# A two-block sequence model in fp32 precision: the second block's branch gates as seven half-width products per unit, and squares summed before the ones-matmul

## The chip, the cores and the metric

One NeuronCore of a Trainium2 chip runs the whole program as one launch. The metric is the device time of the kernel in microseconds (us), lower is better. TensorE (PE) multiplies, VectorE (DVE) and ScalarE (ACT) do elementwise work, GpSimd (POOL) a little of it, and all weights come over one DMA queue that SyncE (SP) fills in program order.

## The reference, cut to what matters

The model is two blocks of two layers each over 528 (first block) or 512 (second block) tokens, width 1024, all fp32. In a layer of the second block, `h = rmsnorm(x, g)` is projected by `w_in`, and three attention branches give `y_a`, `y_b`, `y_m`. The last 3072 columns of `w_in` are the branch gates:

```python
z = jnp.einsum('bsd,dn->bsn', h, w_in)
dq, dk, dv, dg, lq, lk, lv, lg, mq, mg, mgate = jnp.split(z, splits, axis=-1)
...
gates = jax.nn.sigmoid(mgate).reshape(B, S, N_BRANCH, D_MODEL)
merged = gates[:, :, 0] * y_a + gates[:, :, 1] * y_b + gates[:, :, 2] * y_m
return x + jnp.einsum('bsd,de->bse', merged, w_out)
```

Every RMS norm needs, per token, the sum over 1024 channels of `x*x`.

## The kernel before

**Data.** Activations lie channel by channel: xT, hh and hl are eight tiles of 128 channels by 512 (or 528) tokens. hh is the normed activation rounded to the short matmul format, hl the rest. A weight piece is 128 by 1024 fp32, 512 KB. It is staged by DMA in one of two buffers (st), copied by ACT to a rounded half (ch), and DVE subtracts to give the rest (cl). ch and cl have three buffers each. An fp32 product is three matmuls: ch with hh, ch with hl, cl with hh.

**A unit** is 256 output channels: two pieces, the first with input channels 0 to 511, the second with 512 to 1023. `proj` (L339, engine part L1116) computes 128 output channels by 512 tokens: 8 input tiles x 3 matmuls of 512 columns, so a unit is 48 of them. The gates of one layer are 3 branches x 4 units.

**Order.** `Order` writes one list of steps; every engine walks it in that order and runs its own part of each step, waiting on semaphores. Nothing overtakes on an engine. `weights` (L314) puts the conversion of the next piece: SP issues the DMA of the piece two further on (L2717), ACT waits for the staged piece and for the last matmul that read the buffer three pieces back, DVE waits for ACT. Before a unit starts, both of its pieces are converted; during its first half the next piece is put, and behind the matmuls of its second half the one after.

**The second block's layer** (`block2`, L607): differential attention; then three dilated groups g, each with projections (`lq`, `lk`, `lv`) and at its end four score steps `lS` (L1425, L1860, L2438), in which PE takes two pairs of PSUM banks in turn and DVE reads them; then the joint softmax (`lse0` to `lse2`, `pn`); then memory attention (`fA` scores, `fB` transposes, `fC` values, four times each) between the gates of the branches (`lg`, `mg`); then the stage that the change touches. For c = 0 to 3: gates of branch 0, unit c (`gate`, L735; tanh by ACT, L1939, into one of six TG buffers), two `br` steps with pieces "bd" (24 matmuls each), gates of branch 1 and of branch 2, unit c, and two steps with pieces "bm" (two `br` of 12 matmuls each). `brev` (L2583) multiplies and adds in the merge tile. `o2` is the output projection. At c = 0 the copies `ybs` and `yms` (four each on ACT and on DVE) stand behind the gates of branch 1 and 2.

**Start of the second block's layer.** SP loads three bias tables (`gload`, 448 KB each) behind a barrier; the weight pieces that come later stand behind them in the queue.

**Squares** (`squares`, L353). For the norm sums of the three later norms ACT squares each tile (L1571), and PE multiplies it with a ones matrix in plain fp32 (`sqp`, L1106), eight accumulated steps per norm, one behind each output tile.

```python
def weights(self):
    if self.converted < len(self.plan):
        self.put("w", self.converted)
        self.converted += 1
```

Of the kernel before, what the change touches and what calls it, by code (L numbers as in the profile page):

```python
# [290 lines left out]

class Order:


    def __init__(self):
        self.o, self.plan = [], stream_plan()
        self.taken = self.converted = self.sq = self.g = self.gr = self.tg = self.sw = self.rot = 0
        self.owed = False
# [54 lines left out]
    def squares(self, sid):  # L353
        ns = []

# [251 lines left out]
    def block2(self, l):  # L607
        put, nid = self.put, 2 + l
        put("bar", ("b2", l))
        for h in range(3):  # L610
            put("gload", l, h)
        st = {}
# [32 lines left out]
        for g in range(3):  # L645
# [34 lines left out]
            for i in range(4):  # L680
                put("lS", l, g, i)
        put("bar", ("send", l))
# [16 lines left out]
        put("lse2", l)  # L699
        for g in range(3):  # L700
# [26 lines left out]
        def mg(t):  # L727
# [3 lines left out]
            s = self.nsq()  # L731
            tgs["mg", t] = self.ntg()
            put("mgev", l, t, s, tgs["mg", t])
# [18 lines left out]
        gate(0, 0)  # L752
        put("fB", l, 2)
        gate(0, 1)
# [7 lines left out]
        for c in range(4):  # L762
            if c:
                gate(0, 2 * c)
                gate(0, 2 * c + 1)
            for n in (2 * c, 2 * c + 1):
# [3 lines left out]
                if n == 0:  # L770
                    put("fC", l, 3)
                    for t in range(4):
                        put("ymm", l, t, tgs["mg", t])
            gate(1, 2 * c)
            gate(1, 2 * c + 1)
# [3 lines left out]
            gate(2, 2 * c)  # L779
            gate(2, 2 * c + 1)  # L780
            if c == 0:
                for k in range(4):
                    put("yms", l, k)
            if c == 3:
# [4 lines left out]
            for n in (2 * c, 2 * c + 1):  # L789
# [4 lines left out]
                self.weights()  # L794
        for n in (6, 7):
# [7 lines left out]
        for n in range(8):  # L803
            p = first[n] if n < 2 else self.take(2, l, "out", n)
            put("o2", l, n, p, 6 if n < 2 else 0, 8)
            self.weights()
            put("o2ev", l, n)
# [46 lines left out]
def program(nc, I, out):  # L854
    with ExitStack() as ctx:
# [9 lines left out]
        xT, hh = k8(sb("xT", 8 * L)[:, :]), k8(sb("hh", 8 * L, F32R)[:, :])  # L865
        with nc.sbuf_tensor("hn", [128, 8 * L], F32) as HN:
            pass
        hnf, hl = k8(HN[:, :]), k8(sb("hl", 8 * L, F32R)[:, :])
        ifh, ifl = sb("ifh", 128, F32R), sb("ifl", 128, F32R)
        cst, rot_all = sb("cst", S_W), sb("rot", 2 * L)  # L870
        idb = sb("idb", 128, BF16)
        mskb = sb("mskb", C_W - C_MA, BF16)
# [2125 lines left out]
```

## Time and profile before

| | us |
|---|---|
| median of 3 runs | 3013.37 (3012.73 to 3016.75) |
| the profiled execution | 3014.49 |
| its span in the profile | 3012.7 |
| mean granted TensorE clock | 0.99 |
| PE / DVE / ACT busy | 2913.7 / 1620.4 / 1257.1 |

The span is cut into instructions with start and duration; the number in brackets behind a row is how long the engine had stood idle, and which engine's result ended that. Matmuls overlap one another, so that their durations are longer than their spacing: what one costs is the distance from its start to the next start. The difference of 1.8 us between the execution's own time and its span is launch and end.

### The profile page before, as it was taken

To read this page: it belongs to the slowest core of one execution; us is meant where nothing else is said; L and a number is where in the kernel's file an instruction comes from. 1 tells how busy PE (TensorE), PEld (TensorE's weight loads), DVE (VectorE), ACT (ScalarE), POOL (GpSimd) and SP (SyncE) were. 2 spreads that over 40 slices of the span, in tenths; PEclk is the share of its full clock that TensorE was granted. 3 is DMA by queue.
4 is the path that set the end of the run, shared out by engine and by line. 5 is a ranking of instruction groups with operands and counts; after the bars stand their busy time and mean duration, and the time that the engine had idled before them with its cause. 6 is when DMAs were issued, how large, how long until landed. Compare 5 with 4: busy or idle time off the path is not lost.

```text
span 3012.7 us, 42468 instructions
## 1 busy us (share of the span) xinstructions
PE 2913.7 (97%) x17182; PEld 2492.2 (83%) x17182; DVE 1620.4 (54%) x3205; ACT 1257.1 (42%) x2630; POOL 187.2 (6%) x207
## 2 busy tenths in 40 slices
PE   8899999999999999999999999999999999999998
PEld 7888888988887777898888888887888888888886
DVE  6777545367675454676333654334677433565334
ACT  5455423255553233565334333233566324433222
POOL 2100000020001000100000000000100000000000
PEclk9999999999999999999999999999999999999999
DMA  3111222211113222322232222232322232222222
GB/s 116 52 50 54 101 69 71 85 55 57 52 59 107 69 98 91 109 74 78 84 119 85 76 79 84 91 105 91 115 72 80 79 118 84 80 75 86 97 91 84
DMA packets 99726, 250.07 MB, mean 83 GB/s; under 512 B 8597, under 2 KB 44845, under 8 KB 99274
## 3 DMA queue, kind: packets, MB, share of 16 engines
q1 hardware_dynamic: 99530, 247.35, 25.1%
q8 instruction: 136, 2.23, 0.3%
q14 instruction: 60, 0.49, 0.1%
HBM read 239.60 MB, written 6.50 MB: 82 GB/s over the span
## 4 chain that ended last, share of the span: by engine, by line
PE 82%; DVE 9%; ACT 4%; issue 2%; POOL 1%; DMA 1%; SPq 0%; DVEq 0%; POOLq 0%; ACTq 0%
PE ps L93 79%; PE ps L96 3%; ACT Z L99 2%; DVE Z L102 2%; DVE Z L110 2%; DVE cl L102 1%; ACT ch L99 1%; POOL stat L102 1%; DVE ZR L102 1%; DMA st<-in_stream_dram 1%; DVE Z L106 1%; DVE stat L123 1%; DVE stat L110 1%; DVE Z L120 1%; DVE hn L110 0%
## 5 line engine op out<-in xcount | busy, mean ns | idle before, releaser
L93 PE MATMUL ps<-hl,ch 128*128 128x512 f32 (+1 forms) x2512 | 831.5, 359 | 0.0
L93 PE MATMUL ps<-hh,ch 128*128 128x512 f32 (+1 forms) x2368 | 802.5, 365 | 25.5 <-DVE cl L102 10.7
L102 DVE TENSOR_TENSOR cl<-st,ch 128x1024 fp32r<-128x1024 f32 (+1 forms) x436 | 501.9, 1158 | 594.3 <-ACT ch L99 594.0
L93 PE MATMUL ps<-hh,cl 128*128 128x512 f32 (+1 forms) x2368 | 792.5, 361 | 0.0
L99 ACT ACTIVATE ch<-st 128x1024 fp32r<-128x1024 f32 (+1 forms) x436 | 428.7, 990 | 356.9 <-PE ps L93 323.5
L93 PEld LDWEIGHTS ps<-hh,ch 128*128 128x128 f32 x2368 | 423.0, 190 | 107.6 <-ACT Z L99 15.0
L93 PEld LDWEIGHTS ps<-hl,ch 128*128 128x128 f32 x2512 | 448.7, 190 | 72.6
L93 PEld LDWEIGHTS ps<-hh,cl 128*128 128x128 f32 x2368 | 424.0, 190 | 70.7
L99 ACT ACTIVATE Z<-ps 128x512 f32<-128x512 f32 (+7 forms) x506 | 216.4, 437 | 548.5 <-PE ps L93 442.1
L93 PE MATMUL ps<-ZR,ch 128*128 128x512 f32 (+2 forms) x1680 | 443.1, 353 | 2.0 <-DVE cl L102 1.6
L93 PEld LDWEIGHTS ps<-ZR,ch 128*128 128x128 f32 x1680 | 285.0, 189 | 52.3 <-issue 9.2
L93 PE MATMUL ps<-Z 128*128 128x128 f32 (+8 forms) x1522 | 264.2, 317 | 15.1 <-DVE Z L110 5.0
L93 PEld LDWEIGHTS ps<-Z 128*128 128x128 f32 (+5 forms) x1522 | 201.3, 186 | 68.9 <-issue 37.3
L93 PE MATMUL ps<-ZR,cl 128*128 128x512 f32 (+2 forms) x720 | 234.4, 351 | 0.0
L93 PE MATMUL ps<-ch,hh 128*128 128x256 f32 (+2 forms) x736 | 212.4, 289 | 3.8 <-DVE stat L106 2.0
L93 PE MATMUL ps<-cl,hh 128*128 128x256 f32 (+2 forms) x736 | 208.9, 284 | 0.0
L93 PE MATMUL ps<-ch,hl 128*128 128x256 f32 (+2 forms) x736 | 208.3, 283 | 0.0
L99 ACT ACTIVATE Z<-Z,stat 128x512 f32<-128x512 f32 (+4 forms) x264 | 151.2, 587 | 122.2 <-DVE stat L106 113.1
L93 PE MATMUL ps<-ZR 128*128 128x256 f32 (+4 forms) x1040 | 178.1, 331 | 11.1 <-DVE stat L106 11.1
L96 PE MATMUL ps<-cst,Z 128*128 128x128 f32 (+2 forms) x950 | 147.2, 274 | 8.3 <-DVE Z L102 5.9
L99 ACT ACTIVATE Z<-ps,stat 128x272 f32<-128x272 f32 (+2 forms) x160 | 84.2, 532 | 162.5 <-DVE stat L110 128.8
L93 PEld LDWEIGHTS ps<-ZR 128*128 128x128 f32 (+2 forms) x1040 | 122.7, 189 | 30.9 <-DVE stat L106 12.5
(133 smaller groups left out, 3183.5 us busy)
## 6 DMA issues: line engine op xcount, KB each, us to landing
st<-in_stream_dram SPq DMA_DIRECT2D x372, 512.0 KB, 3.5
st<-in_stream_dram SPq DMA_DIRECT2D x64, 256.0 KB, 3.2
Z<-decay_rows SPq DMA_DIRECT2D x8, 904.0 KB, 5.4
Z<-bias_lines SPq DMA_DIRECT2D x16, 448.0 KB, 3.6
ya_spill<-Z SPq DMA_DIRECT2D x8, 512.0 KB, 4.0
Z<-ya_spill SPq DMA_DIRECT2D x2, 2048.0 KB, 7.9
Z<-in_x_dram SPq DMA_DIRECT2D x4, 512.0 KB, 5.4
Z<-in_mem_dram SPq DMA_DIRECT2D x2, 1024.0 KB, 6.4
```

The source lines that it names most:

```text
L93: return Ins(self, self.e and self.e.matmul(o, a, b, start=start, stop=stop, skip_group_check=True))
L96: return Ins(self, self.e and self.e.transpose(o, a, i))
L99: return Ins(self, self.e and self.e.activation(o, i, f, **kw))
L102: return Ins(self, self.e and self.e.tensor_tensor(o, a, b, op))
L106: return Ins(self, self.e and self.e.tensor_scalar(o, a, s1, s2, op0))
L110: return Ins(self, self.e and self.e.scalar_tensor_tensor(out=o, in0=a, scalar=s, in1=b, op0=op0, op1=op1))
L120: return Ins(self, self.e and self.e.tensor_copy(o, i))
L123: return Ins(self, self.e and self.e.tensor_reduce(o, i, X, op, negate=negate))
```

## The change

Each 256-channel gate unit is computed as a 2 x 2 block product in seven multiplications (Strassen's scheme) in place of eight. W is split in input halves and output halves (A11, A21, A12, A22), the activation in input halves and token halves. One product (`fp`) has 4 input tiles x 3 matmuls of 256 columns.

- DVE forms S1 = A21+A22, S2 = S1-A11, S3 = A11-A21, S4 = A12-S2 on staged weights (128 x 512 each). The seven factors A11, S2, A12, S3, S1, A22, S4 are converted one by one (`cv`, half a buffer each).
- The activation's four combinations need fp32 values again: `tpn` normalises xT in place (8 x 512, behind `lS` of groups 0 and 1), `tpc` subtracts (4 x 1024, around `lS` of group 2), `tph`/`tpl` split them (two behind `lse2`, two ahead of the first gate unit). So x is saved to DRAM at the layer's start (`xsp`, 8 DMAs of 256 KB) and read back at c = 3 (`xld`).
- `fe` sums the products: ACT copies one and applies tanh to the others, DVE adds the partial sums that lie in PSUM.
- Conversions are put by halves of a buffer (`halves`), one half behind each product, with six halves in the ring; the factor S4 counts as two.
- TG goes from six to four buffers, `br` takes banks 3, 4, 5, and gate, bd and bm pieces use a third staging buffer.
- For the three later norms DVE adds the squares of tiles 0 to 6 (`sqs`), and PE does two ones-matmul steps in place of eight.

```diff
+PRODUCTS = ("A11", "S2", "A12", "S3", "S1", "A22", "S4")
+N_STAGE, N_HALVES = 3, 6
...
+def halves_of(task):
+    return 1 if task[0] == "cv" and task[2] < 6 else 2
...
     def weights(self):
-        if self.converted < len(self.plan):
-            self.put("w", self.converted)
-            self.converted += 1
+        self.halves(2)
+
+    def halves(self, n):
+        self.room += n
+        while self.at < len(self.tasks) and halves_of(self.tasks[self.at]) <= self.room:
+            t = self.tasks[self.at]
+            self.put(*t)
+            self.room -= halves_of(t)
+            self.at += 1
...
     def squares(self, sid):
         ns = []
+        if sid:
+            ns += [self.nsq(), self.nsq()]
+            def total(k):
+                if k < 7:
+                    self.put("sqa", sid, k, ns[k > 0])
+                    if k:
+                        self.put("sqs", sid, k, ns)
+                else:
+                    self.put("sqp", sid, 0, ns[0])
+                    self.put("sqa", sid, 7, ns[1])
+            def end():
+                self.put("sqp", sid, 7, ns[1])
+            return total, end
...
         for h in range(3):
             put("gload", l, h)
+        put("xsp", l)
...
             for i in range(4):
                 put("lS", l, g, i)
+                if g < 2:
+                    put("tpn", l, 4 * g + i)
+                elif i:
+                    put("tpc", l, i - 1)
+        put("tpc", l, 3)
...
         put("lse2", l)
+        for x in range(2):
+            put("tph", l, x)
+            put("tpl", l, x)
...
-        def gate(bi, n):
-            if n % 2 == 0:
-                st["u"] = self.unit(2, l, 10240 + 1024 * bi + 128 * n)
-            self.proj(("gt", l, bi, n), nid, 512, st["u"], n % 2)
-            tgs[bi, n] = self.ntg()
-            put("gtev", l, bi, n, tgs[bi, n])
+        def gates(bi, c, beside=lambda j: None):
+            u = self.unit(2, l, 10240 + 1024 * bi + 256 * c)[0]
+            tgs[bi, 2 * c], tgs[bi, 2 * c + 1] = tg = self.ntg(), self.ntg()
+            n = self.nsq()
+            for j in range(7):
+                put("fp", l, bi, c, u, j)
+                if j:
+                    put("fe", l, bi, c, j - 1, n, *tg)
+                    self.halves(1)
+                beside(j)
+            put("fe", l, bi, c, 6, n, *tg)
+            self.halves(2)
...
         put("fC", l, 1)
         put("fA", l, 3)
-        gate(0, 0)
-        put("fB", l, 2)
-        gate(0, 1)
+        for x in (2, 3):
+            put("tph", l, x)
+            put("tpl", l, x)
+        gates(0, 0, lambda j: put("fB", l, 2) if j == 3 else None)
         put("fC", l, 2)
         put("fB", l, 3)
...
+            def fp(l, bi, c, u, j):
+                key, b = ("fs", l, bi, c), (0, 1, 0, 1, 2, 1, 2)[j]
+                opens = j in (0, 1, 4)
+                if opens:
+                    pe.wait_ge(*held[b])
+                    held[b] = [("free", key, b)]
+                elif j == 2:
+                    pe.wait_ge(("p1", *key))
+                elif j == 3:
+                    pe.wait_ge(("u2", *key))
+                elif j == 5:
+                    pe.wait_ge(("u3", *key))
+                else:
+                    pe.wait_ge(("c22", *key))
+                if j in (1, 3, 4, 5):
+                    pe.wait_ge(("T", l, {1: 0, 3: 1, 4: 2, 5: 3}[j]))
+                pe.wait_ge(("cl", u, j))
+                (wh, wl), (xh, xl), o = product(u, j), MOVING[j], bank(b)[:, 0:256]
+                for k in range(4):
+                    pe.matmul(o, wh[:, k, :], xh[:, k, :], opens and k == 0, False)
+                    pe.matmul(o, wh[:, k, :], xl[:, k, :], False, False)
+                    m = pe.matmul(o, wl[:, k, :], xh[:, k, :], False, k == 3)
+                m.then_inc("pe_fast", ("full", key, j), ("wfree", u, j))
```

On ACT:

```diff
+            def cv(u, j):
+                act.wait_ge(*ring_before[u, j])
+                act.wait_ge(("st", u + (j > 0)) if j in (0, 2, 5) else ("S", u, j))
+                act.activation(product(u, j)[0], source(u, j), ACT.Copy).then_inc("act_whi", ("ch", u, j))
...
+            def fe(l, bi, c, e, n, ta, tb):
...
+                if e == 0:
+                    act.wait_ge(("full", key, 0), *sqw(n))
+                    act.activation(s[:, 0:256], bank(0)[:, 0:256], ACT.Copy).then_inc("act_fast", ("p1", *key))
+                elif e == 2:
...
+                elif e == 5:
+                    act.wait_ge(("c21", *key), ("c22", *key))
+                    act.activation(TG[tb % 4], TG[tb % 4], ACT.Tanh, scale=0.5).then_inc(
+                        "act_fast", ("gt", l, bi, 2 * c + 1))
+                elif e == 6:
+                    act.wait_ge(("c12", *key))
```

On DVE:

```diff
+            def fe(l, bi, c, e, n, ta, tb):
...
+                if e == 1:
+                    dve.wait_ge(("full", key, 1), ("p1", *key))
+                    dve.tensor_tensor(u2, r6, p1, ALU.add).then_inc("dve_fast", ("u2", *key))
...
+                elif e == 5:
+                    dve.wait_ge(("full", key, 5), *tgw(l, tb))
+                    dve.tensor_tensor(h[:, 0:256], r6, p1, ALU.add).then_inc("dve_fast", ("free", key, 1), ("c21", *key))
```

On SP:

```diff
+            def xsp(l):
+                sp.wait_ge(*[("o2e", 0, n) if l else ("o1e", 1, n) for n in range(8)])
+                for k in range(8):
+                    sp.dma_start(x_dram[l][:, 512 * k:512 * k + 512], xT[:, k, NM:L]).then_inc(
+                        "d_xs", *([("xs", l)] if k == 7 else []), by=16)
```

The parts `tpn`, `tpc`, `tph` and `tpl` are one DVE or ACT instruction per step; `cv` on DVE forms the sums (two for j = 0, one for j = 1 ahead of and one for j = 2 behind the subtraction) and then subtracts as for a whole piece.

## Rows read from the trace of the kernel before

**Rows 1.** The page: busy time, share of the span and instructions of each engine.

```profile
PE 2913.7 (97%) x17182; PEld 2492.2 (83%) x17182; DVE 1620.4 (54%) x3205; ACT 1257.1 (42%) x2630; POOL 187.2 (6%) x207
```

**Rows 2.** Windows, first layer's gate stage: PE, PEld, DVE, ACT, POOL busy, clock, DMA, GB/s.

```profile
1841.00:2043.00 202.00, 202.00 (x866) 162.06 (x865) 79.77 (x91) 58.90 (x75) 0.00 (x0) 1.00 0.30 100
```

**Rows 3.** Timeline, half-width projection of differential attention: first and last of 24 PE rows.

```profile
1293.72 0.28 PE L93 MATMUL ps<-ch,hh 128*128 128x256 f32 x1
...
1296.43 0.28 PE L93 MATMUL ps<-ch,hl 128*128 128x256 f32 x1
```

**Rows 4.** Timeline, first block's output projection: two successive ones-matmul steps.

```profile
1126.21 1.02 PE L93 MATMUL ps<-sq,ones 128*128 128x512 f32 x2
...
1138.24 1.02 PE L93 MATMUL ps<-sq,ones 128*128 128x512 f32 x2
```

**Rows 5.** Groups by form: DVE and ACT durations; columns are count, busy us, mean ns.

```profile
L102 DVE TENSOR_TENSOR cl<-st,ch 128x1024 fp32r<-128x1024 f32 x372 | 459.2, 1238 | 552.9 <-ACT ch L99 552.8
L102 DVE TENSOR_TENSOR cl<-st,ch 128x512 fp32r<-128x512 f32 x64 | 42.7, 690 | 41.4 <-ACT ch L99 41.2
L102 DVE TENSOR_TENSOR ZR<-ps,ZR 128x256 fp32r<-128x256 f32 x16 | 6.7, 419 | 1.9 <-ACT ZR L99 1.9
...
L99 ACT ACTIVATE ch<-st 128x1024 fp32r<-128x1024 f32 x372 | 390.8, 1054 | 338.3 <-PE ps L93 322.7 <-DMA st<-in_stream_dram 14.3
L99 ACT ACTIVATE ch<-st 128x512 fp32r<-128x512 f32 x64 | 37.9, 620 | 18.6 <-DMA st<-in_stream_dram 17.3 <-PE ps L93 0.8
L99 ACT ACTIVATE Z<-ps 128x256 f32<-128x256 f32 x62 | 23.4, 377 | 31.2 <-PE ps L93 30.7
```

**Rows 6.** Timeline, gate stage: hand-over from PE to ACT at a projection's end.

```profile
1930.09 0.40 PE L93 MATMUL ps<-hh,ch 128*128 128x512 f32 x1
...
1930.29 0.60 ACT L99 ACTIVATE Z<-ps 128x512 f32<-128x512 f32 x1 [10.16 <-PE ps L93]
```

**Rows 7.** Timeline, DVE: three independent instructions in a row, then a dependent pair.

```profile
1823.06 1.90 DVE L102 TENSOR_TENSOR ZR<-Z,ZR 128x512 fp32r<-128x512 f32 x3 [0.46 <-ACT ZR L99]
...
1972.15 0.69 DVE L110 SCALAR_TENSOR_TENSOR Z<-Z,ps 128x512 f32<-128x512 f32 x1 [3.21 <-PE ps L93]
1972.87 0.69 DVE L102 TENSOR_TENSOR Z<-Z 128x512 f32<-128x512 f32 x1
```

**Rows 8.** Timeline, PE: the first projection behind the score steps of group 0.

```profile
1545.26 0.50 PE L93 MATMUL ps<-hh,ch 128*128 128x512 f32 x1 [0.16 <-DVE stat L113]
```

**Rows 9.** Timeline, DMA queue, ACT and PE at the second block's start.

```profile
1209.25 1.29 SPq L132 DMA_DIRECT2D Z<-bias_lines  x3
...
1218.62 1.39 ACT L99 ACTIVATE ch<-st 128x512 fp32r<-128x512 f32 x2 [5.37 <-DMA st<-in_stream_dram]
...
1220.12 0.47 PE L93 MATMUL ps<-hh,ch 128*128 128x512 f32 x1 [2.54 <-DVE cl L102]
```

**Rows 10.** The page: DMA issues, count, KB each, us from issue to landing.

```profile
Z<-ya_spill SPq DMA_DIRECT2D x2, 2048.0 KB, 7.9
```

**Rows 11.** Timeline, DVE behind the joint softmax.

```profile
1731.11 1.23 DVE L102 TENSOR_TENSOR cl<-st,ch 128x1024 fp32r<-128x1024 f32 x1 [1.13 <-ACT ch L99]
1733.38 0.69 DVE L110 SCALAR_TENSOR_TENSOR Z<-sq,ps 128x512 f32<-128x512 f32 x1 [1.04 <-ACT sq L99]
```

**Rows 12.** Timeline, PE, ACT and DVE around the last memory score step.

```profile
1806.86 0.58 PE L93 MATMUL ps<-hh,ch 128*128 128x512 f32 x1
...
1810.23 0.21 ACT L99 ACTIVATION_READ_ACCUMULATOR Z<-ps,stat 128x1 f32 x1
...
1810.48 0.18 DVE L126 RECIPROCAL stat<-stat 128x4 f32<-128x4 f32 x1 [2.00 <-ACT Z L99]
```

**Rows 13.** Windows around PE's idle times: columns as in the windows above.

```profile
1215.00:1220.00 5.00, 2.57 (x12) 1.73 (x10) 0.69 (x1) 1.26 (x2) 0.25 (x1) 1.00 0.43 123
...
1720.00:1725.00 5.00, 5.00 (x16) 3.92 (x15) 4.93 (x6) 0.00 (x0) 4.07 (x3) 0.62 0.66 213
...
2130.00:2135.00 5.00, 3.13 (x12) 2.32 (x11) 2.76 (x4) 2.45 (x4) 2.05 (x4) 0.84 0.31 90
```

More of the change, by code:

```diff
@@ L290, in half_piece, with fast_piece, conversions, weight_ring @@
     return blk == 2 and what == "in" and x < 2048
+PRODUCTS = ("A11", "S2", "A12", "S3", "S1", "A22", "S4")
+N_STAGE, N_HALVES = 3, 6
+def fast_piece(r):
+    blk, _, what, x, _ = stream_plan()[r]
+    return blk == 2 and what == "in" and x >= 10240
+def conversions():
+    o, plan = [], stream_plan()
+    for r in range(len(plan)):
+        if not fast_piece(r):
+            o.append(("w", r))
+        elif plan[r][4] == 0:
+            o.extend([("cv", r, j) for j in range(7)])
+    return o
+def halves_of(task):
+    return 1 if task[0] == "cv" and task[2] < 6 else 2
+def weight_ring():
+    at, owner, before = {}, [], {}
+    for t in conversions():
+        at[t[1:]] = len(owner)
+        real = 1 if t[0] == "cv" else 2
+        waits = []
+        for h in range(len(owner), len(owner) + real):
+            g = h - N_HALVES
+            while g >= 0 and owner[g] is None:
+                g -= N_HALVES
+            if g >= 0 and ("wfree", *owner[g]) not in waits:
+                waits.append(("wfree", *owner[g]))
+        before[t[1:]] = waits
+        owner += [t[1:]] * real + [None] * (halves_of(t) - real)
+    return at, before
+def stage_ring():
+    plan, buf, prev, latest = stream_plan(), [], [], {0: -2, 1: -1, 2: -3}
+    for r, (blk, l, what, x, h) in enumerate(plan):
+        wide = fast_piece(r) or what in ("bd", "bm")
+        b = min((0, 1, 2) if wide else (0, 1), key=lambda i: latest[i])
+        buf.append(b)
+        prev.append(latest[b] if latest[b] >= 0 else None)
+        latest[b] = r
+    return buf, prev
 class Order:
@@ L763, in block2 @@
             if c:
-                gate(0, 2 * c)
-                gate(0, 2 * c + 1)
+                gates(0, c)
             for n in (2 * c, 2 * c + 1):
@@ L772, in block2 @@
                     for t in range(4):
-                        put("ymm", l, t, tgs["mg", t])
-            gate(1, 2 * c)
-            gate(1, 2 * c + 1)
+                        put("ymm", l, t)
+            gates(1, c)
             if c == 0:
@@ L778, in block2 @@
                     put("ybs", l, k)
-            gate(2, 2 * c)
-            gate(2, 2 * c + 1)
+            gates(2, c)
             if c == 0:
@@ L783, in block2 @@
                     put("yms", l, k)
+            if c == 3:
+                put("xld", l, 0, 2)
             if c == 3:
@@ L806, in block2 @@
             self.weights()
+            if n == 0:
+                put("xld", l, 6, 8)
             put("o2ev", l, n)
@@ L1056, in program @@
         PMT = [z(2048 + 1024 * i, 1024) for i in range(2)]
-        TG = [z(22528 + 512 * i, 512) for i in range(6)]
+        TG = [z(22528 + 512 * i, 512) for i in range(4)]
         nm_, dm_ = stat[:, 8:24], stat[:, 24:40]
@@ L2620, in vector_program @@
                       lse1=lse1, lse2=lse2, pn=pn, lgev=lgev, lgm=lgm, eT=eT, eP=eP, yasp=yasp, ybs=ybs, yms=yms,
-                      mgs=mgs, fA=fA, fB=fB, fC=fC, mgev=mgev, ymm=ymm, brev=brev, o2ev=o2ev, turn=turn, final=final,
+                      mgs=mgs, fA=fA, fB=fB, fC=fC, mgev=mgev, cv=cv, tpn=tpn, tpc=tpc, tpl=tpl, fe=fe, ymm=ymm, brev=brev, o2ev=o2ev, turn=turn, final=final,
                       bar=dve.bar)
@@ L2735, in consts @@
             def consts():
-                for r in range(NST):
-                    piece(r)
+                pieces(done)
                 sp.dma_start(ifs, I["w_if"]).then_inc("d_consts", by=16)
```

195 lines of the change are left out of this document (151 added, 44 removed).

## Prediction, on record before the changed kernel ran

> **What bounds the kernel now.** The busy shares come first: TensorE works in 97% of the span, DVE in 54% [rows 1]. The windows of the gate stage show why the change is aimed there: PE is busy in all 202.00 us, at clock 1.00, 866 matmuls in 202 us, so one of 512 columns costs 0.233 us; DVE has 79.77 us of work, ACT 58.90 [rows 2]. Whatever leaves PE there shortens the run, and whatever makes PE wait lengthens it, as nothing makes up for it later. A unit of gates is 48 x 0.233 = 11.19 us.
>
> **Products.** A half-width matmul is in the trace: 24 start 2.71 us apart from first to last, 2.71/23 = 0.118 us each [rows 3]. A unit becomes 7 x 12 = 84 of them, 9.90 us; one product takes 1.41 us. Saving 1.29 us x 24 units = -31.0 us. The Trainium skill (TensorE: Matmul & The Clock Gate, Back-to-back issue gap) has a rule against this: in a stream of weight-load and matmul pairs a matmul of 128 columns takes about 81 ns and one of 512 about 131, so halving the columns does not halve the time. An estimate on a line between its two figures puts 256 columns at 98 ns, a unit at 6.3 us before and 8.2 after, and the change's products at +46 us. The rows show 0.118 against 0.233, so the trace does not agree, and I go by the rows.
>
> **Squares.** Two successive ones-steps start 12.03 us apart [rows 4] with 48 matmuls between, 11.19; a step costs 0.84 us. Six fewer in three norms: 18 x 0.84 = -15.1 us. The six DVE additions stand beside 11 us of matmuls per tile and the last ones-step still waits for the last square only: nothing more.
>
> Together -46.1 us. Now what is added, with the durations of the groups by form [rows 5]: on DVE 0.69 for 512 columns from SBUF, 0.42 for 256 from PSUM, 1.24 for 1024; on ACT 0.62, 0.38, 1.05. PE's end is seen by another engine 0.20 us after the next matmul's start [rows 6]. Independent DVE instructions of 512 follow at 0.61 (three in 1.90), dependent ones at 0.72 [rows 7].
>
> **Preparing the activations.** `tpn` stands on DVE between the score steps. PE already waited 0.16 us there for DVE to free the banks of step 2 [rows 8], so the two `tpn` ahead of that are all delay: 2 x 0.66 = 1.3 us in groups 0 and 1, and one dependent `tpc` of 1.24 in group 2: 3.9 us a layer, 7.8. The other subtractions are covered by the 11 us of the next unit. The two splits behind `lse2` delay DVE by 2.3 us ahead of `pn`; DVE idles 1.13 and 1.04 there before PE needs the result [rows 11], so they cost nothing; without that cover 2.3 a layer.
>
> **Saving x.** `xsp` puts 2 MB on the queue behind the bias tables and ahead of weight pieces. That stretch is the one in which transfers already decide: ACT waited 5.37 us for a piece and PE 2.54 [rows 9]. Nothing like these stores is shown there; 2 MB in one issue land in 7.9 us [rows 10]. Bounds: 0 (stores beside loads) and 9.8 (2.1 MB at the 213 GB/s of a busy window [rows 13]). I take 7.9, as the queue has one order: 15.8 us. Reading back at c = 3 goes beside 40 us of matmuls at a DMA share of 0.30 [rows 2]: nothing.
>
> **First gate unit.** ACT's order is: exps of the last score step, two `tph`, then the copy that product 2 waits for. The projection starts at 1806.86, the exps end at 1810.44 [rows 12], 3.6 us later; two copies of 1.05 and one of 0.38 give 6.1, where two products end at 2.8: PE stands 3.3. DVE's two `tpl`, a factor and the sum that product 3 waits for end 0.5 later than PE comes: 3.8 us, 7.6 in two layers.
>
> **Unit to branch matmul.** This is the largest term. Before, the next stage's first piece is converted while PE is in the first half of the unit. Now a unit starts with four halves ahead (factors 0 to 3). The halves put behind products 1 to 4 go to factors 4, 5 and 6 (two), so the piece of `br` has its two halves only at product 6, behind `fe` 5. On ACT `fe` 5 waits for DVE's sum of product 5. From that product's end: 0.20, DVE 0.42, ACT's tanh, whose successor starts 0.52 later, the conversion 1.05, DVE 1.24, four hand-overs of about 0.04 (1810.44 to 1810.48 [rows 12]): 3.56 us. PE has product 6 in the meantime, 1.41. It stands 2.15 us. That happens behind branch 0 and branch 2 of every c; at c = 0 branch 0 has `fC` and `fB` behind it (0.4 left), and `yms` adds 0.8: 7 x 2.15 + 1.2 = 16.2 a layer, 32.4.
>
> **Unit to unit.** Behind branch 1, factors 1, 2, 3 of branch 2 are put behind `fe` 5 and 6. ACT's conversion of factor 1 waits for the tanh, DVE's `fe` 6 for that conversion, the next tanh for `fe` 6, and so on back and forth. Followed with the same durations from the end of product 4 of branch 1: DVE does `fe` 4 (0.2), S1 and S2 (to 1.9), factor 0 and `fe` 5 (to 2.9); ACT tanh, factor 1 (3.5 to 4.1); DVE factor 1 (4.8): product 1 starts at 4.9, where PE was free at 4.24. DVE `fe` 6 (5.1), ACT tanh, factors 2 and 3, the copy of product 0 (7.0): product 2 starts at 7.05 instead of 6.3. DVE factor 2, S4, factors 3 and 4, `fe` 1 (6.2 to 9.0): product 3 at 9.1 instead of 8.45. Together 2.0 us. At c = 0 the four `ybs` pairs lie between (4 x 0.54 on ACT, 4 x 0.61 on DVE), which puts the copy 2.2 later and `fe` 1 0.9 behind that: 4.4. A layer 10.4, both 20.8.
>
> **Branch matmul to unit.** The other way round DVE has `brev` (to 1.7 behind "bm"), factors 2 to 4 and S4 (4 x 0.61) and `fe` 1 ahead of product 3: 4.6, where PE comes at 3 x 1.41 = 4.24: 0.4 late, three times. Behind "bd" `brev` is one instruction and DVE is in time, but at c = 0 four `ymm` stand ahead: 0.8. A layer 2.0, both 4.0. Four TG buffers suffice, since `brev` frees them a stage earlier; the third staging buffer only lengthens a piece's lead; POOL has nothing in this stage.
>
> **Clock.** A wait of PE can pull the granted clock down. Of idle times near 2 us, one of 2.43 (2.57 busy of 5) left it at 1.00 and one of 1.87 came with 0.84; behind two close together it was 0.62, with 16 matmuls in 5 us where 21 fit, 1.3 us lost [rows 13]. I count it behind the two long waits at the layers' start, 2.6, and bound the rest by 0 and 22 x 1.3 = 28.
>
> **Sum.** -46.1 + 7.8 + 15.8 + 7.6 + 32.4 + 20.8 + 4.0 + 2.6 = +44.9 us on the profiled execution's 3014.49; that one lies 1.1 above the median of 3013.37, so 3058 us.
>
> **Rivals.** A (forecast, 0.62): as above, 3058.
> B (0.09), faster: the order of conversions does not reach PE. Its place is the slot of the `br` piece and of factors 1 to 3; its price is the 57.2 us of the last three stage terms; it decides if ch and cl of that piece stand before product 6 ends. For it: the totals fit, 11 x 0.61 + 5 x 0.42 = 8.8 us a unit on DVE and 6.1 on ACT, against PE's 9.9. Against: the in-order engines. 3058 - 57 = 3001. With nothing added anywhere it would be 2967.
> C (0.14): the clock falls at every wait of 2 us: 3058 + 26 = 3084. For it the 0.84, against it the 1.00 [rows 13].
> D (0.10): the stores run beside the loads, so 15.8 goes: 3042.
> E (0.02): half-width matmuls do not cost half, because every one brings a weight load; against it [rows 3], where the load is hidden at 0.118 and each matmul has a load of its own. At most it would take the 0.233 of a full-width one: 2016 x 0.115 = +232, 3290. It would then be a change that doesn't do what it says. The rule of the Trainium skill cited above points this way.
> The remaining 0.03 are waits I have not found.
>
> **Numbers.** The range takes D with some of the small waits halved (3025) and C with some clock loss more (3090): 3025 to 3090. About 0.2% (6 us) is what a measurement of this kernel can tell from no change. Faster 0.07 (most of B), within it 0.03, slower 0.90.
>
> **What would show it.** In the profile after: matmuls of 256 columns from ch with hh at a spacing of 0.118; 12 fewer ones-rows in each of the norms; PE idle of about 2.1 us "by DVE cl" ahead of `br`, 14 times, with ACT's conversion behind a tanh; idle ahead of products 1 to 3 of branch 2; one idle of about 10 us at each start of the second block's layers, ended by a transfer; DVE near 0.8 busy in the gate stage, PE under 0.9. Wrong the prediction would be if the gate stage of a layer had PE at 1.00 and were 15 us shorter; the step that failed would then be the slot of the conversions. If only the start of the layer shows no new idle time, the step is the queue.

## The result, and the profile after

The changed kernel takes 3065.61 us (median of 4, 3062.21 to 3067.44) against 3014.23 for the kernel before (3012.73 to 3016.75): ratio 1.0168, 95% interval 1.0151 to 1.0186, 51 us slower. The prediction was 3058, in 3025 to 3090: right in sign and range, 6 to 8 us short; as will be seen, the clock in the gate stage was left out, and smaller terms hid half of that. The profiled run took 3067.44 us, its span is 3065.7.

The page of the changed kernel first, its busy line (PE, PEld, DVE, ACT, POOL), as in [rows 1], and the two PE groups with the most idle time:

```profile
PE 2895.6 (94%) x17998; PEld 2519.2 (82%) x17998; DVE 1810.6 (59%) x3591; ACT 1318.9 (43%) x2806; POOL 187.2 (6%) x207
...
L93 PE MATMUL ps<-hh,ch 128*128 128x512 f32 (+2 forms) x2368 | 759.3, 347 | 55.7 <-DVE cl L102 22.9
...
L93 PE MATMUL ps<-ZR,ch 128*128 128x512 f32 (+2 forms) x1680 | 444.1, 354 | 33.0 <-DVE cl L102 30.2
```

PE went from 97% to 94% of a longer span. The second group holds the branch matmuls; 30.2 of its 33.0 us of idle time are ended by the low part of a converted weight piece. Next the windows of the changed kernel, with the columns of [rows 2]: the start of the second block's first layer, two stretches behind waits in the gate stage, one without, and the stage as a whole.

```profile
1200.00:1205.00 5.00, 5.00 (x24) 4.03 (x23) 1.94 (x3) 1.19 (x2) 2.39 (x4) 1.00 0.99 262
1205.00:1210.00 5.00, 2.01 (x9) 1.30 (x7) 0.00 (x0) 0.00 (x0) 0.00 (x0) 0.98 1.05 390
1210.00:1215.00 5.00, 1.10 (x3) 0.94 (x4) 1.85 (x3) 2.43 (x4) 0.54 (x1) 0.50 0.41 129
1215.00:1220.00 5.00, 5.00 (x13) 3.85 (x12) 1.61 (x3) 1.20 (x3) 1.85 (x4) 0.50 0.48 125
1892.00:1896.00 4.00, 4.00 (x12) 3.12 (x12) 1.23 (x1) 1.17 (x2) 0.00 (x0) 0.57 0.61 171
1988.00:1992.00 4.00, 4.00 (x12) 3.09 (x12) 1.34 (x2) 1.39 (x2) 0.00 (x0) 0.57 0.52 159
2024.00:2028.00 4.00, 4.00 (x36) 4.00 (x35) 3.83 (x7) 1.42 (x3) 0.00 (x0) 1.00 0.23 20
1852.00:2054.00 202.00, 179.51 (x1135) 160.08 (x1136) 128.90 (x214) 76.46 (x138) 0.00 (x0) 0.97 0.29 91
```

Where [rows 2] had PE busy in all of 202.00 us at clock 1.00, it is busy in 179.51 at 0.97; DVE is busy in 128.90, a share of 0.64. At 1892 and 1988 the clock is 0.57: PE made 12 matmuls in 4 us, where 17 of 0.233 fit. The layer's start shows the 2 MB of stores and the loads behind them at 390 GB/s, then a starved PE, then the lower clock level. The timeline of the changed kernel there:

```profile
1198.67 1.28 SPq L132 DMA_DIRECT2D Z<-bias_lines  x3
...
1200.24 4.48 SPq L132 DMA_DIRECT2D x_spill<-xT  x8
...
1212.39 1.39 ACT L99 ACTIVATE ch<-st 128x512 fp32r<-128x512 f32 x2 [9.72 <-DMA st<-in_stream_dram]
...
1213.90 0.77 PE L93 MATMUL ps<-hh,ch 128*128 128x512 f32 x1 [6.89 <-DVE cl L102]
```

The bias tables are issued 10.58 us earlier than in [rows 9] (1209.25): two norms' squares. PE's wait is 6.89 us where it was 2.54. Then the gate stage. The next rows are of the changed kernel, from its timeline in the first layer: PE's waits, one of each kind.

```profile
1811.05 0.58 PE L93 MATMUL ps<-hh,ch 128*128 128x256 f32 x1 [3.28 <-ACT Z L99]
...
1855.99 0.39 PE L93 MATMUL ps<-hh,ch 128*128 128x256 f32 x1 [2.43 <-ACT sq L99]
...
1883.07 0.38 PE L93 MATMUL ps<-crr,ch 128*128 128x256 f32 x1 [0.19 <-DVE sq L102]
...
1915.92 0.36 PE L93 MATMUL ps<-crr,ch 128*128 128x256 f32 x1 [0.51 <-DVE cl L102]
1917.95 0.36 PE L93 MATMUL ps<-hh,ch 128*128 128x256 f32 x1 [0.39 <-ACT sq L99]
1920.00 0.38 PE L93 MATMUL ps<-crr,ch 128*128 128x256 f32 x1 [0.40 <-DVE sq L102]
1928.00 0.70 PE L93 MATMUL ps<-ZR,ch 128*128 128x512 f32 x2 [2.05 <-DVE cl L102]
```

And the chain behind one of the 2.05, DVE and ACT ahead of a branch matmul:

```profile
1887.62 0.42 DVE L102 TENSOR_TENSOR Z<-ps,sq 128x256 f32<-128x256 f32 x1 [1.00 <-PE ps L93]
1888.08 0.63 ACT L99 ACTIVATE Z<-Z 128x512 f32<-128x512 f32 x1 [4.26 <-DVE Z L102]
1888.62 1.04 ACT L99 ACTIVATE ch<-Z 128x1024 fp32r<-128x1024 f32 x1
1889.69 1.23 DVE L102 TENSOR_TENSOR cl<-Z,ch 128x1024 fp32r<-128x1024 f32 x1 [1.64 <-ACT ch L99]
...
1891.06 0.70 PE L93 MATMUL ps<-ZR,ch 128*128 128x512 f32 x2 [2.05 <-DVE cl L102]
```

This is the chain of the prediction: DVE's sum of product 5, the tanh, the high part, the low part, PE. ACT had been idle for 4.26 us before that tanh, and the SP queue had issued this piece at 1869.27, 19 us before: it is an order, not a lack of time.

### The profile page after: what moved, and what is told of

The parts are those of the page before. It is cut to its first block, busy times and chain, and to the rows that moved or that the text cites. A ratio compares the mean times of both kernels' runs of the same rounds, so it can differ in the third digit from the quotient of the medians.

```text
span 3065.7 us, 45001 instructions
## 1 busy us (share of the span) xinstructions
PE 2895.6 (94%) x17998; PEld 2519.2 (82%) x17998; DVE 1810.6 (59%) x3591; ACT 1318.9 (43%) x2806; POOL 187.2 (6%) x207
## 4 chain that ended last, share of the span: by engine, by line
PE 74%; DVE 15%; ACT 6%; issue 3%; POOL 1%; DMA 1%; SPq 1%; DVEq 0%; POOLq 0%; ACTq 0%
PE ps L93 71%; DVE cl L102 3%; PE ps L96 3%; DVE Z L102 3%; ACT Z L99 2%; ACT ch L99 2%; DVE Z L110 2%; DVE ZR L102 1%; DVE stat L123 1%; SPq L132 1%; DVE Z L106 1%; DVE Z L120 1%; DVE Z L113 1%; DVE hn L110 1%; POOL stat L102 1%
## 5 line engine op out<-in xcount | busy, mean ns | idle before, releaser
L93 PE MATMUL ps<-hh,ch 128*128 128x512 f32 (+2 forms) x2368 | 759.3, 347 | 55.7 <-DVE cl L102 22.9
L93 PE MATMUL ps<-hl,ch 128*128 128x512 f32 (+2 forms) x2512 | 789.1, 342 | 0.0
L93 PE MATMUL ps<-hh,cl 128*128 128x512 f32 (+2 forms) x2368 | 749.6, 343 | 0.0
L102 DVE TENSOR_TENSOR cl<-st,ch 128x1024 fp32r<-128x1024 f32 (+1 forms) x458 | 483.3, 1062 | 448.8 <-ACT ch L99 447.7
L99 ACT ACTIVATE ch<-st 128x1024 fp32r<-128x1024 f32 (+1 forms) x458 | 415.1, 915 | 271.7 <-PE ps L93 231.6
L93 PE MATMUL ps<-ZR,ch 128*128 128x512 f32 (+2 forms) x1680 | 444.1, 354 | 33.0 <-DVE cl L102 30.2
L93 PEld LDWEIGHTS ps<-ZR,ch 128*128 128x128 f32 x1680 | 286.7, 191 | 81.5 <-issue 32.7
L99 ACT ACTIVATE Z<-ps 64x128 f32<-64x128 f32 (+6 forms) x482 | 196.7, 418 | 360.4 <-PE ps L93 251.0
L93 PE MATMUL ps<-Z 128*128 128x128 f32 (+8 forms) x1522 | 266.7, 319 | 15.5 <-DVE Z L110 4.5
L99 ACT ACTIVATE sq<-ps 128x128 f32<-128x128 f32 (+3 forms) x152 | 65.4, 430 | 210.7 <-PE ps L93 210.5
```

Source lines behind the costliest of these rows:

```text
L93: return Ins(self, self.e and self.e.matmul(o, a, b, start=start, stop=stop, skip_group_check=True))
L99: return Ins(self, self.e and self.e.activation(o, i, f, **kw))
L102: return Ins(self, self.e and self.e.tensor_tensor(o, a, b, op))
```

## Experiments

Each is compared with the kernel before on the same chip. No part of the computation is left out in any of them.

**e1_squares.** The squares' part alone, in the kernel before:

```diff
+        if sid:
+            ns += [self.nsq(), self.nsq()]
...
+                    self.put("sqa", sid, k, ns[k > 0])
+                    if k:
+                        self.put("sqs", sid, k, ns)
```

> The kernel before with the change's first part alone: the second, third and fourth norms' seven tiles' squares are summed on DVE and PE takes six ones steps fewer at each of three norms of two layers' worth (48 fewer ones records). The theory of the prediction prices them at 18 steps of 0.84 us, -15.1 us, and nothing given back, since the additions on DVE lie beside the projections: about 2999 us against 3014 before. Rival: the sum over tiles ends later than the single squares did, and PE waits for it ahead of the ones step at each norm (1 to 2 us for each of three): about 3003 to 3005. The first bias load of the second block's first layer, which came 10.6 us earlier in the changed kernel with two of the three norms behind it, should do so here too.

2998.38 us, ratio 0.9937 (0.9922 to 0.9952); against its own before of 3015.52 that is 17 us less, 14 to 24 by the interval. The predicted 15.1 lies in it, and nothing is given back. The bias tables of the first layer are issued at

```profile
1200.95 1.29 SPq L132 DMA_DIRECT2D Z<-bias_lines  x3
```

8.3 us earlier than in [rows 9], and not 10.6 as expected. The first block's clock accounts for the difference: each shortfall from 1.00 in the windows of 4 us up to 1200, times 4 us, sums to 18.7 us here and to 15.4 in the changed kernel. All the loss, and more than the 51 us, is the part of the gate units and of what they need: 3065.6 - 2998.4 = 67 us.

**e3_store.** The saving of x in eight steps beside the attention, in the changed kernel:

```diff
-        put("xsp", l)
...
+            if 12 <= s < 20:
+                put("xsp", l, s - 12)
             if 0 <= s - 2 < 32:
                 put("dB", l, s - 2)
```

> The changed kernel with the saving of x (2 MB on SP's queue) taken out of the layer's start and made in eight parts beside the attention's steps of the same layer. Theory, the saving holds up the pieces of the in-projection behind it on the queue (6.9 us waits at each layer's start where there were 2.5 and 1.9 before) and the clock at half for some 10 us behind it comes of that wait: -4.5 us a layer from the wait and -3 us a layer from the clock, -13 to -16 us, 3050 to 3053 us. Rival, the wait is that for the preceding norm's end and what is behind it, and only 4 to 5 us a layer come from the queue, the clock falling all the same: -9 us, 3057. Second rival, the parts hold up the transfers beside the attention: nothing gained, 3065 or more.

3048.13 us, ratio 1.0111 (1.0094 to 1.0128): 17.5 us less than the changed kernel's 3065.6, slightly over the upper end expected. In its timeline and windows:

```profile
1207.89 0.47 PE L93 MATMUL ps<-hh,ch 128*128 128x512 f32 x1 [1.12 <-DVE cl L102]
```

```profile
1205.00:1210.00 5.00, 3.88 (x17) 2.91 (x16) 2.76 (x4) 2.45 (x4) 1.27 (x3) 1.00 0.38 115
1210.00:1215.00 5.00, 5.00 (x23) 4.02 (x23) 2.03 (x3) 2.45 (x4) 1.12 (x2) 1.00 0.54 169
```

The wait falls from 6.89 to 1.12 (e1_squares, which saves nothing, has 1.16 there), in the second layer from 6.82 to 0.96, and the clock stays at 1.00. Waiting makes 11.6 of the 17.5 us in two layers; the other 6 are the matmuls that ran at 0.50 behind it (13 in the 5 us from 1215, where a window of e3_store has 23). No cost of the stores beside the attention is seen. Rival D of the prediction, that they run beside the loads where the change put them, is out.

**e4_tpn.** The activations' preparation behind all four score steps of its group:

```diff
             for i in range(4):
                 put("lS", l, g, i)
+            for i in range(4):
                 if g < 2:
                     put("tpn", l, 4 * g + i)
-                elif i:
-                    put("tpc", l, i - 1)
-        put("tpc", l, 3)
+                else:
+                    put("tpc", l, i)
```

> The changed kernel with the eight multiplications and four differences on DVE that make the products' activations put behind all four score steps of their group, not between them. The prediction priced them at 1.3 + 1.3 + 1.24 us a layer, 7.8 us in all, as far as PE waits behind them. Landmarks of the changed kernel gave about 1.1 + 1.2 + 1.2 us a layer. Theory: the wait goes and nothing comes in its place, -7 us, 3059 us. Rival: DVE's time has to be spent somewhere in this stretch, and the next projection's split waits by as much: no change, 3066.

3059.67 us, ratio 1.0142 (1.0127 to 1.0157), 5.9 less than the changed kernel, though the intervals of the two overlap. The rows carry it better. The first projection behind group 0 waits again as in [rows 8]; the first fence is of the changed kernel, the second of e4_tpn:

```profile
1542.61 0.50 PE L93 MATMUL ps<-hh,ch 128*128 128x512 f32 x1 [0.67 <-DVE stat L113]
```

```profile
1540.05 0.50 PE L93 MATMUL ps<-hh,ch 128*128 128x512 f32 x1 [0.16 <-DVE stat L113]
```

With these 0.51 us go two waits of 0.54 at the end of group 1 and one of 1.15 at the end of group 2: 2.7 us a layer, 5.5 in two.

**e2_lead and e6_lead1.** The conversions of the gate stage begun earlier, by two half-pieces or by one:

```diff
                 if j:
                     put("fe", l, bi, c, j - 1, n, *tg)
-                    self.halves(1)
+                self.halves(1 if j else 2)
                 beside(j)
             put("fe", l, bi, c, 6, n, *tg)
-            self.halves(2)
```

That is e2_lead; e6_lead1 has `self.halves(1)` at every product and `self.halves(1)` behind the last `fe`. In both, DVE's first sum of a unit also waits for the last reading of that sum's tile by the unit before, which is long done.

> The changed kernel with the gate units' conversions begun two half-pieces earlier: the two that stand behind the last product now stand behind the first, so that the branch piece's low part stands on DVE ahead of the sums of the last two products, and four of the next unit's products are converted before it begins, not two. The theory of the prediction, in which the wait for that low part is the cost (2.05 us shown, with 0.16 us of pace 2.2 us, 14 times in two layers: 31 us), then unit to unit (0.5 + 0.4 + 0.4, with pace 1.8 us, 10 times: 18 us) and the clock that falls behind these waits (some 6 us a layer by the windows at 0.57): -40 to -60 us, 3006 to 3026 us. Rival one, DVE and ACT have too much to do in this stage, whatever the order (DVE near 0.8 busy): the waits only move to other products, -5 to -15 us, 3050 to 3060. Rival two, the wait is ACT's tanh and not the order: half of the wait ahead of the branch matmuls stays (1.0 us), 3030 to 3040.

3046.78 us, ratio 1.0095 (1.0079 to 1.011): 19 less, a miss, between the theory and its rivals. The waits of 2.05 are gone, others have come; in e2_lead's timeline, the DMA queue, DVE and PE in the unit behind branch 1:

```profile
1906.44 0.33 SPq L132 DMA_DIRECT2D st<-in_stream_dram  x1
...
1909.96 0.69 DVE L102 TENSOR_TENSOR cst<-st 128x512 f32<-128x512 f32 x1 [1.41 <-issue]
...
1911.89 0.42 DVE L102 TENSOR_TENSOR stat<-ps,sq 128x256 f32<-128x256 f32 x1
...
1912.37 0.39 PE L93 MATMUL ps<-hl,ch 128*128 128x256 f32 x1 [1.25 <-DVE stat L102]
```

DVE reaches the next unit's first sum 1.41 us too early. The row names no releaser (`issue`), but the times fit the transfer: the weight piece was issued at 1906.44 and the page gives a median of 3.5 us to landing, which ends at 1909.94. Behind DVE's wait stands the unpacking for which PE waits. The order was too eager. (What comes next counts the waits of e2_lead a little off: the 1.25 us stand ahead of a unit's sixth product, and the 0.79 us inside the unit behind a branch, not ahead of the branch matmuls, which wait only once, 1.28 us at c = 0.)

> The changed kernel with the gate units' conversions begun one half-piece earlier, not two. In e2_lead the waits ahead of the branch matmuls fell from 2.05 to 0.79 us, but new ones of 1.25 us came ahead of the seventh product and stayed at 1.01 us ahead of the next unit: there the first sum of the next unit stands on DVE ahead of the unpacking of the fourth product, and starts only when its half-piece, issued 3.5 us earlier, has landed (DVE idle 1.41 us). Theory: the order is right by one half-piece, the transfer has landed when DVE comes to it, and the branch piece's first part still stands ahead of the second tanh: no new wait, the ones ahead of the branch matmuls and of the next unit under 0.5 us, -35 to -50 us, 3015 to 3030. Rival, that the two half-pieces more or less only trade one wait for the other: as e2_lead or worse, 3045 to 3055. Second rival, DVE's own work in this stage is the bound: -10 to -15 us, 3050 to 3055 us.

3034.6 us, ratio 1.0076 (1.0061 to 1.0091): 31 less than the changed kernel, 12 less than e2_lead. The wait for the transfer is gone from all of the first layer's gate units but one: at c = 0 DVE still waits 1.34 us for it ahead of a unit's first sum, and PE 1.38 behind that (1848.73). No wait is left ahead of the branch matmuls but one of 1.07 at c = 0. The clock is low in the first layer's stage only in two windows around 1856 (0.68, 0.89). It missed the expected 35 to 50 mainly by a wait that grew, ahead of the third product of a next unit (from 0.39 to 1.61, at c = 0 from 2.43 to 3.69); ACT and PE of e6_lead1:

```profile
1913.48 0.42 ACT L99 ACTIVATE Z<-Z 128x256 f32<-128x256 f32 x1 [1.70 <-DVE Z L102]
1913.80 0.61 ACT L99 ACTIVATE ch<-st 128x512 fp32r<-128x512 f32 x1
1914.32 0.61 ACT L99 ACTIVATE ch<-cst 128x512 fp32r<-128x512 f32 x1
...
1914.84 0.36 ACT L99 ACTIVATE sq<-ps 128x256 f32<-128x256 f32 x1
...
1915.25 0.38 PE L93 MATMUL ps<-hh,ch 128*128 128x256 f32 x1 [1.61 <-ACT sq L99]
```

The copy that frees the bank stands behind a tanh for which ACT waited 1.70 us, and then behind two conversions, one of them for a product that comes later. Inside the unit behind a branch a wait grew too, from 0.19 to 0.78.

**e8_first.** The last memory score step ahead of the projection half before the gates:

```diff
         put("fB", l, 1)
+        put("fA", l, 3)
         mg(3)
         put("fC", l, 1)
-        put("fA", l, 3)
```

> The changed kernel with the fourth block of the memory attention's scores put ahead of the last half of the projection before the gates, not behind it, so that the gate units' first product finds its banks read out by ACT (3.3 us wait at the first gate unit in either layer, with the clock at 0.75 to 0.82 behind it). Theory: the wait goes and the clock stays, -3.4 us and -1.5 us a layer: -8 to -10 us, 3056. Rival: the products' activations, whose high parts ACT makes behind the exponentials, are late too, so that the wait goes to the second product: -2 us, 3064.

3060.96 us, ratio 1.016 (1.0146 to 1.0174): by its interval not to be told from the changed kernel. The first unit's wait went from 3.28 <-ACT to

```profile
1812.04 0.39 PE L93 MATMUL ps<-hh,ch 128*128 128x256 f32 x1 [2.12 <-DVE Z L110]
```

so neither theory nor rival: the wait went to another releaser at the same matmul, and 1.2 us of waiting a layer were won. The clock was not: the window from 1812 to 1816 is at 0.59.

**e7_all1.** e3_store, e4_tpn, e6_lead1 and e8_first in one.

> All four mends in the changed kernel: the saving of x beside the attention, the activations' preparation behind the score steps, conversions one half-piece earlier, the scores ahead of the last projection half. If the theory holds, that the change's own work is a gain (-31 us in PE's products, -15 us in ones steps) and that what it lost lies in waits that order alone makes, their sum is -17.5 (e3_store) - 5.9 (e4_tpn) - 35 to -50 (e6_lead1) - 8 (e8_first): 2985 to 3000 us, under the 3014 before and about as fast as the squares alone (2998) or faster. If e6_lead1's rival holds, it is 3015, no better than before. That the single gains do not add, because a wait taken away in one place comes back at the next on the same engine, would give 3020 to 3035.

3012.68 us, ratio 0.9997 (0.9988 to 1.0006): 53 us less than the changed kernel, where the single gains sum to 17.5 + 5.9 + 31.0 + 4.7 = 59. They add, all but 6 us. Of the 13 us that are missing to 3000, these are 6; e6_lead1 had missed its least by 4 and e8_first by 3.

**e9_slots and e10_slots2.** e7_all1 with the conversions placed by product, and the four `ybs` beside products 2 to 5:

```diff
-                self.halves(1)
+                self.halves((0, 1, 1, 2, 1, 1, 1)[j])
...
-            if c == 0:
-                for k in range(4):
-                    put("ybs", l, k)
-            gates(2, c)
+            gates(2, c, lambda j: put("ybs", l, j - 2) if c == 0 and 2 <= j < 6 else None)
```

That is e9_slots; e10_slots2 has (0, 1, 1, 2, 1, 2, 0) in that place.

> e7_all1 with two more moves in the gate stage. In e7_all1 PE still waits 1.6 us <-ACT sq ahead of each next unit's third product, six times a layer in e6_lead1's and its pattern's rows (1.6 us and, at the first, 3.7): on ACT the copy that frees the first product's bank stands behind two conversions of the unit's later products, and at the first also behind four high parts of the mixer's output. Here the later conversions stand behind that copy (no half-piece at the first product, two at the fourth), and the four high parts stand beside four of the products. Theory, the queue order on ACT is the wait: 3 x 1.6 + 3.7 + pace 0.16 each = 9 us a layer, with 2 to 3 us of clock, and part of the 0.8 us ahead of the next unit behind a branch (3 a layer): -18 to -26 us, 2987 to 2995, under the before and under the squares alone (2998). Rival, the bank is free but the product's own low part on DVE is as late: the wait changes its releaser (<-DVE cl) and stays, -4 us or less, 3009. Rival two, the conversions put later are late for the fifth product: a new wait of 1 us a unit, 24 us, no gain or slower, 3010 to 3020.

2996.55 us, ratio 0.9939 (0.9925 to 0.9953), 16 less than e7_all1, just short of the 18 to 26 expected. The waits on the bank fell from 1.6 to 1.1, the first from 3.70 to 1.11, those inside the unit behind a branch from 0.79 to 0.19, and the clock's loss of 3.4 us in e7_all1's first stage is gone.

> e9_slots with the next unit's third half-piece converted at the sixth product and not at the seventh. In e9_slots PE waits 1.1 us <-ACT sq at the third product of each next unit: the copy that frees the first product's bank is held on ACT by the last tanh, which waits for DVE's sum, which stands behind a low part whose high part ACT made behind the first tanh. Theory: with the third conversion ahead of that tanh the chain is shorter by a hand-over, and the wait falls from 1.1 to 0.5 us or less, 10 times in two layers: -5 to -8 us, 2989 to 2992. Rival: the last tanh follows the seventh product's end by the same chain anyway: within 1 us of e9_slots, 2996. Rival two, the conversion ahead is late for the branch pieces or waits for its transfer as in e2_lead: slower, 3000 to 3005.

2989.25 us, ratio 0.9905 (0.9891 to 0.9919), 7 less than e9_slots, as expected: 26 us under its before, the fastest of the study, below the kernel before, the changed kernel and the squares alone. No wait between units is marked any more. The whole list of PE's marked waits of this kernel from 1780 to 2050, and its window of the stage:

```profile
1799.95 0.39 PE L93 MATMUL ps<-hh,ch 128*128 128x256 f32 x1 [2.17 <-DVE Z L110]
...
1836.85 0.38 PE L93 MATMUL ps<-hh,ch 128*128 128x256 f32 x1 [1.69 <-DVE Z L102]
...
1852.78 0.70 PE L93 MATMUL ps<-ZR,ch 128*128 128x512 f32 x2 [1.07 <-DVE ZR L102]
...
1865.85 0.39 PE L93 MATMUL ps<-crr,ch 128*128 128x256 f32 x1 [0.19 <-DVE sq L102]
...
1919.33 0.39 PE L93 MATMUL ps<-crr,ch 128*128 128x256 f32 x1 [0.18 <-DVE sq L102]
...
1972.72 0.38 PE L93 MATMUL ps<-crr,ch 128*128 128x256 f32 x1 [0.19 <-DVE sq L102]
```

```profile
1840.00:2042.00 202.00, 200.02 (x1252) 177.98 (x1251) 144.06 (x233) 86.17 (x152) 0.90 (x2) 1.00 0.36 113
```

DVE has 144 us of work in these 202, 0.71, and PE stands 2 us by the window: DVE's load was never the bound.

**e11_gates.** e9_slots without the squares' part: the gate units alone, in their better order.

> e9_slots without the change's squares: the seven-product units alone, with all that was mended in their order, and the second, third and fourth norms' squares single as before. Theory, the two parts add: the squares alone took 15 to 17 us off, so this is 2996.6 + 16 = 3012 to 3014, the time of before: the units' 31 us less of products are used up by the waits and paces that the unpacking still makes (16 us idle a layer in a stretch where there was none). Rival, the gate part is worth more by itself, because the squares' sums load DVE where the units do: 3005 or less.

3011.59 us, ratio 0.9985 (0.9976 to 0.9994), against 0.9939 with the squares. The parts add (0.9985 x 0.9937 = 0.9922; the measured 0.9939 is within the intervals), and the seven-product units with all that they need are worth 4 us here, though their products alone save 30 (see below): waits take back nearly all of it. By e10_slots2 against e1_squares (0.9905 against 0.9937) the best order found makes them worth about 9.

## Why the prediction was right, and where it was off

**Products: right.** The prediction took 0.118 us from a stream of 24 half-width matmuls [rows 3] and gave a unit 84 x 0.118 = 9.90 us. A unit of the changed kernel in which PE waits for nothing, its first matmul and the first of the next unit:

```profile
1963.13 0.28 PE L93 MATMUL ps<-hh,ch 128*128 128x256 f32 x1
...
1973.07 0.28 PE L93 MATMUL ps<-hh,ch 128*128 128x256 f32 x1
```

9.94 us for 84 matmuls, 0.118 each; another such unit, from 1903.88, takes 9.95. So a unit saves 11.19 - 9.95 = 1.24 us, and 24 units 30 us. The ratio 0.118 to 0.233 is a half within 2%, so rival E is out. The prediction's estimate from the rule of the Trainium skill (TensorE: Matmul & The Clock Gate, Back-to-back issue gap) would have made the products cost 46 us; these rows don't agree with it.

In the faster orders a unit seems dearer. Two units in succession in e10_slots2, with no marked wait, and what lies between two products of the first:

```profile
1989.73 0.28 PE L93 MATMUL ps<-hh,ch 128*128 128x256 f32 x1
...
1998.04 0.42 DVE L102 TENSOR_TENSOR Z<-ps,stat 128x256 f32<-128x256 f32 x1
...
1998.11 0.28 PE L93 MATMUL ps<-hl,cl 128*128 128x256 f32 x1
1998.52 0.39 PE L93 MATMUL ps<-hh,ch 128*128 128x256 f32 x1
1998.74 0.28 PE L93 MATMUL ps<-hl,ch 128*128 128x256 f32 x1
...
2010.41 0.63 PE L93 MATMUL ps<-ZR,ch 128*128 128x512 f32 x2
```

They take 20.68 us, 10.34 a unit. The last product of the first unit waits for DVE's sum of product 4, which ends at 1998.46. Its first matmul starts 0.06 us later, 0.41 behind the one ahead of it instead of 0.118, and the second follows at 0.22. The same happens at 2003.02, 0.06 behind ACT's copy, and at 2004.60, 0.05 behind DVE's sum. Nearly all of the 0.86 us above 168 x 0.118 stands at these three places: they are waits too short to be marked, and the price of the products is not touched by them. Counted from start to start, marked and unmarked waits cost e10_slots2 about 10 us in the first layer's stage and 9 in the second's. Of the 30 us saved that leaves about 11, near the 9 that it gains on e1_squares.

**Squares: right,** 15.1 against 14 to 24 (e1_squares).

**Preparing the activations: right in place, a little too dear.** 7.8 against 5.9 (e4_tpn).

**Saving x: right in sum.** 15.8, with 2.6 for the clock, against 17.5 (e3_store). The make-up was other than the row of 7.9 us [rows 10] suggested: waiting takes 11.6, the low clock behind it 6, and the idle of about 10 us named as a sign is one of 6.89. Stores and loads together went at a higher rate than the 213 GB/s of the bound, and ACT's first piece behind the stores came late (9.72 us of idle, ended by the DMA).

**The waits in the gate stage: right.** The marked waits of the changed kernel's first layer, from its rows in 1803 to 2055, sum to 27.0 us. A mark leaves part of the loss out: the branch matmul marked 2.05 starts 2.21 us later than the stream's spacing would have it, and the first matmul of a product behind a wait takes 0.22 us to the next one and not 0.118. From start to start, as the prediction had followed them, the 25 waits cost 32.7 us, against 32.4 forecast. By kind, as predicted, marked, and from start to start: first unit 3.8, 3.28, 3.5; unit to branch matmul 16.2, 15.5 (1.96 + 6 x 2.05, and 0.60 and 0.62 at c = 0), 17.6; unit to unit 10.4, 7.7 (3.7 at c = 0, then 1.30, 1.32, 1.30), 10.6; branch matmul to unit 2.0, 0.55, 1.3. That the sums agree within 1% is partly chance, as the kinds differ by up to 1.4 us. That their cause is the slot, as rival B's test had it, is shown by e6_lead1: the branch waits went when the piece stood ahead of `fe` 5. B itself is out: the order did reach PE. One sign did not come: DVE is 0.64 busy in the stage, not near 0.8.

**Clock: the term that was mis-sized.** The prediction counted two drops of 1.3 us at the layers' start and none in the gate stage; its bound was 28 us, with C at 0.14. From the SP queue's rows, the stretch from the load of `ya_spill` to the next layer's bias tables takes 2140.78 - 1762.60 = 378.2 us in the changed kernel and 2106.90 - 1752.82 = 354.1 in e1_squares. Of these 24.1 us the waits make +32.7 and the products -14.9 (12 x 1.24), which leaves 6.3 for the clock. The windows of 4 us between 1800 and 2060, each shortfall from 1.00 times 4 us, sum to 6.8, those of the second layer's stage (2748 to 3004) to 6.8 too. Thus some 13 to 14 us in two layers, half way to C: the clock fell behind some waits of about 2 us, not behind all.

The sum by measured terms: products -30, squares -17, activations +6, saving +17.5 (with the clock at the layers' start), waits 33 and 32 (the second layer's from its marks, 26.1, and the same addition a wait), clock in the stage +14: about +55 against 51.4, so 3 to 4 us stay unaccounted for. The stage's clock alone would have put the prediction 14 us too low. Against that stand squares, activations and saving, together 5 us better than priced, and the unaccounted rest: that 3058 came within 8 us of 3065.6 is partly luck.

Of the waits that e10_slots2 keeps, the 2.17 us ahead of the first unit is what e8_first's move had left. The 1.69 us stands ahead of the last product of branch 1 at c = 0, and behind a DVE that idles for 1.53 us ahead of the next unit's first sum, as in e2_lead: there the weight piece is still too late. Whether they can be ordered away was not tried.

## What to carry to other kernels

An engine that is full and has no wait gains from less arithmetic only if every in-order queue that feeds it keeps its lead: before the code is written, follow for each new consumer where its producer's instruction stands on ACT and DVE, and what that queue waits for just ahead of it. All of the 51 us lost here and 25 more (3065.6 to 2989.3) came back by moving steps, with no instruction less. Too early is as bad as too late: a conversion placed before its transfer has landed blocks the unpacking behind it. And what a wait costs is to be read from start to start: a marked wait here cost about 0.2 us more than its mark on average, and waits too short for a mark took nearly 3 us in a stage that seemed to have almost none.

## What the runs showed of the hardware that was not expected

- The clock behind short waits is not settled by the wait's length. In the changed kernel's first gate stage six waits of 2.05 and one of 1.96 us precede branch matmuls; the 4 us windows behind three of them are at 0.57, 0.57 and 0.69, behind the other four at 1.00. In e3_store, whose stage is the same but 10 us earlier, it is low behind the same three (0.76, 0.71 and 0.69), and so in e4_tpn (0.68, 0.62 and 0.77). But in e8_first, 1.6 us later than in the changed kernel, it is low behind two of these waits only (0.60 at 1928, 0.78 at 1988), one of them another than before, and also behind the 2.42 at c = 0 (0.64 at 1856). Behind the first unit's 3.3 us it fell in the changed kernel (0.82, 0.75) but not in e6_lead1 nor in e3_store; behind 3.7 it fell in e6_lead1; behind 6.9 it was at 0.50 in the windows from 1210 to 1220. In e10_slots2, whose longest wait of this stage is 2.17, every window of the first layer's stage is at 1.00; behind the same first wait in the second layer (2.14) one is at 0.57. What decides between them is not shown.
- Eight stores of 256 KB on one queue, with the loads behind them, moved 390 GB/s in a 5 us window, against 262 in the one ahead of it.
- At three short hand-overs of e10_slots2 the matmul started 0.05 to 0.06 us after the DVE or ACT instruction that it waited for had ended, and the matmul behind it 0.22 us later, where the stream has 0.118. The timeline marks no idle time for such a hand-over when it is short (0.15 us is the smallest mark met in these traces), so that 10.34 us for a unit looked like dearer matmuls, where the matmuls alone take 9.94.
